# Attention block of a two-block layer on one NeuronCore: value products swapped, on divided probabilities, heads in pairs

## Chip, cores and metric

One core of a Trainium2 chip. The metric is the device time of one execution in microseconds (us), lower is better. The work is in float32, batch 1, 256 tokens, width 2048.

## What is computed

Two blocks, one behind the other. The first has gated linear attention, a convolution branch and a feed-forward layer. The change lies in the second block, and there in its attention of 32 heads of 64: heads 0 to 15 with a T5 bias and dilated masks, 16 to 31 with a neighbourhood bias. With 256 tokens both become a full softmax over 256 keys with a bias and mask.

```python
h = x @ w_in_2                      # q, k, v, gate for heads A and heads B
s = q @ k.T * 64 ** -0.5 + bias     # per head, 256 x 256
p = exp(s - max(s)); den = p.sum(-1)
y = (p @ v / den) * silu(gate)
x = layer_norm(2 ** 0.25 * x + y @ w_out_2) * gain + shift
```

## The kernel before

**Units and steps.** All weight products are cut into 96 units of 512 output columns. A unit has 4 steps of 512 rows each, 384 steps in all (`UNITS`, `NS`). A step s is 24 matmuls of TensorE (`products`, L1190 to L1192): 4 blocks of 128 rows, 2 token tiles, and three products of high and low parts (x_lo w_hi, x_hi w_lo, x_hi w_hi) in fp32r. The weights come by SP's queue into `raw` (three buffers, one load of 1 MB a step). `split(s)` makes `whi` on ScalarE (L604) and `wlo = raw - whi` on VectorE (L849). Each engine does split(s + 2) first in step s, and then the jobs of step s, in order. SP loads step s + 3 after VectorE's split of s.

**Jobs.** `jobs(s)` lists what else a step does. TensorE runs it behind the step's 24 products. `post(u)`, at the last step of unit u, evicts its accumulators `acc`. `turn_...` transposes 8 tiles of the result through two of the four `side` banks of PSUM; ScalarE takes the high part (L609), VectorE the low part (L856). The four banks go round in the order of use: `take` waits until the bank's use four places back has been read.

**Attention.** Units q2, k2, v2 of four groups g (8 heads each) stand at steps 304 to 351, then gates y (352 to 367) and out (368 to 383). Job `att` a runs at 316 + 12 g + (a - 8 g), then a = 32 and 33 at steps 360 and 361. An even a scores heads a and a + 1 (`scores`, L1259 and L1263, three split products with 64 rows each, the two heads in two halves of the array). VectorE adds the bias (L1150) and takes the maximum (L1154, L1157), ScalarE the Exp (L825), in place in `Sm`. Each step a then transposes head a - 1 (`probs`, L1273, 4 tiles in plain f32), ScalarE copies it to `PT` (L820), and the values of head a - 2 follow (`values`, L1286): four plain f32 matmuls, stationary PT (128 x 128), moving `v1`, 64 columns of v and one column of ones that gives the denominator. VectorE divides (L1135, L1138) into `Y`. The gate's post takes Silu on ScalarE (L672), VectorE multiplies by Y (L979), and the product is turned into `A_hi` and `A_lo`. TensorE's order in a step is values, probs, scores, then a turn.

**POOL** fetches the bias of heads a + 2 and a + 3 (`fetch_bias`) after the scores of the same buffer have been read: 2 DMAs (heads below 16) or 4 (L506), then adds the mask (L509).

## Time and profile before

| | us |
|---|---|
| median of 3 runs (2280.4 to 2281.58) | 2281.12 |
| the profiled execution | 2281.08 |
| its span | 2279.3 |
| TensorE busy | 2263.3 (99%) |
| TensorE weight load busy | 1881.8 (83%) |
| VectorE, ScalarE, GpSimd busy | 1215.5, 963.6, 201.0 |

TensorE's granted clock is 0.998 of full. Matmul ends are modelled, so the time that a matmul takes in the stream is read from one start to the next. PE is TensorE, PEld its weight load, DVE VectorE, ACT ScalarE, POOL GpSimd.

### The profile page before, as it was taken

Reading aid. Unit: us, or ns where it says so; the run is one execution under the profiler, and the core shown is the slowest. Engines: PE = TensorE matmul, PEld = TensorE weight load, DVE = VectorE, ACT = ScalarE, POOL = GpSimd, SP = SyncE. Lnnn points to the kernel's source line nnn. Section 1 sums busy time; section 2 is a strip of 40 time slices with the busy share of each in tenths; the row PEclk is TensorE's granted clock in tenths of the full one; section 3 lists DMA queues with packets and bytes.
Section 4 is the critical chain, followed back from the end, with each engine's and each line's share of the span. In section 5 each row is a group of like instructions: output and inputs, shape, how many; then the busy total and the mean of one; then the engine's idle time right before and its main releaser. Section 6 shows DMA issues by size and latency. Waiting matters only on the chain.

```text
span 2279.3 us, 24818 instructions
## 1 busy us (share of the span) xinstructions
PE 2263.3 (99%) x10648; PEld 1881.8 (83%) x10648; DVE 1215.5 (53%) x971; ACT 963.6 (42%) x832; POOL 201.0 (9%) x204
## 2 busy tenths in 40 slices
PE   9999999999999999999999999999999999999997
PEld 7888878888888888888888888888888888888886
DVE  5456535545555544555454454544455555665656
ACT  6444454433344343344433433433444444444532
POOL 1003100000000000000000000000000122253201
PEclk9999999999999999999999999999999999999999
DMA  8545446676666666655555565555556655655663
GB/s 273 185 133 163 148 149 203 194 213 202 202 197 202 204 202 205 219 192 182 192 190 188 186 196 188 184 192 196 185 184 202 243 192 172 189 165 179 211 231 111
DMA packets 213533, 435.60 MB, mean 191 GB/s; under 512 B 8596, under 2 KB 9328, under 8 KB 212528
## 3 DMA queue, kind: packets, MB, share of 16 engines
q1 hardware_dynamic: 205600, 408.98, 55.0%
q0 software_dynamic: 7680, 24.98, 4.6%
q8 instruction: 84, 1.38, 0.2%
q14 instruction: 25, 0.20, 0.0%
q10 hardware_dynamic: 144, 0.07, 0.0%
HBM read 421.93 MB, written 12.06 MB: 190 GB/s over the span
## 4 chain that ended last, share of the span: by engine, by line
PE 98%; DVE 1%; DMA 1%; POOL 0%; ACT 0%; issue 0%; SPq 0%; POOLq 0%; DVEq 0%; ACTq 0%
PE acc L1190 30%; PE acc L1191 30%; PE acc L1192 30%; PE side L1200 2%; PE side L1230 1%; PE side L1286 1%; PE side L1273 1%; PE side L1259 1%; DMA bia<-rb_scratch 0%; DVE X L1018 0%; DVE X L1014 0%; DMA X<-in_x 0%; POOL bia L509 0%; PE side L1350 0%; POOL bia L506 0%
## 5 line engine op out<-in xcount | busy, mean ns | idle before, releaser
L849 DVE TENSOR_TENSOR wlo<-raw,whi 128x2048 fp32r<-128x2048 f32 x382 | 891.4, 2333 | 816.0 <-ACT whi L604 816.0
L604 ACT ACTIVATE whi<-raw 128x2048 fp32r<-128x2048 f32 x382 | 731.6, 1915 | 769.0 <-PE acc L1192 769.0
L1190 PE MATMUL acc<-whi,setA_lo 128*128 128x512 f32 x1792 | 704.4, 393 | 0.1
L1191 PE MATMUL acc<-wlo,setA_hi 128*128 128x512 f32 x1792 | 698.8, 390 | 0.0
L1192 PE MATMUL acc<-whi,setA_hi 128*128 128x512 f32 x1792 | 698.6, 390 | 0.0
L1190 PE MATMUL acc<-whi,setB_lo 128*128 128x512 f32 x1280 | 503.5, 393 | 0.0
L1191 PE MATMUL acc<-wlo,setB_hi 128*128 128x512 f32 x1280 | 498.4, 389 | 0.0
L1192 PE MATMUL acc<-whi,setB_hi 128*128 128x512 f32 x1280 | 498.2, 389 | 0.0
L1190 PEld LDWEIGHTS acc<-whi,setA_lo 128*128 128x128 f32 x1792 | 337.4, 188 | 71.3 <-issue 1.8
L1192 PEld LDWEIGHTS acc<-whi,setA_hi 128*128 128x128 f32 x1792 | 337.3, 188 | 70.3
L1191 PEld LDWEIGHTS acc<-wlo,setA_hi 128*128 128x128 f32 x1792 | 337.4, 188 | 69.4 <-issue 1.0
L1192 PEld LDWEIGHTS acc<-whi,setB_hi 128*128 128x128 f32 x1280 | 240.3, 188 | 50.2
L1190 PEld LDWEIGHTS acc<-whi,setB_lo 128*128 128x128 f32 x1280 | 240.4, 188 | 49.7
L1191 PEld LDWEIGHTS acc<-wlo,setB_hi 128*128 128x128 f32 x1280 | 240.5, 188 | 47.9
L550 POOL TENSOR_TENSOR tmp<-tmp 128x1024 f32<-128x1024 f32 x16 | 30.3, 1896 | 753.5 <-DVE tmp L968 753.5
L609 ACT ACTIVATE setA_hi<-side 128x512 fp32r<-128x512 f32 x48 | 26.1, 595 | 76.6 <-PE side L1200 76.6
L509 POOL TENSOR_TENSOR bia<-bia,msk 128x512 f32<-128x512 f32 x32 | 48.4, 1514 | 81.2 <-DMA bia<-rb_scratch 42.5
L856 DVE TENSOR_TENSOR setA_lo<-side,setA_hi 128x512 fp32r<-128x512 f32 x48 | 30.9, 687 | 38.4 <-ACT setA_hi L609 38.4
L820 ACT ACTIVATE PT<-side 128x512 f32<-128x512 f32 x32 | 19.1, 598 | 75.5 <-PE side L1273 75.5
L1200 PE MATMUL side<-ident,tmp 128*128 128x128 f32 x384 | 49.9, 273 | 0.5 <-DVE Y L1138 0.5
L1200 PEld LDWEIGHTS side<-ident,tmp 128*128 128x128 f32 x384 | 44.4, 140 | 6.7 <-issue 0.7
L543 POOL TENSOR_TENSOR DD<-cum 128x2048 f32<-128x2048 f32 x8 | 33.3, 4161 | 184.6 <-DVE cum L1058 120.6
(181 smaller groups left out, 938.0 us busy)
## 6 DMA issues: line engine op xcount, KB each, us to landing
raw<-in_w_in SPq DMA_DIRECT2D x190, 1024.0 KB, 5.2
raw<-in_w_ffn_up SPq DMA_DIRECT2D x64, 1024.0 KB, 5.3
raw<-in_w_ffn_down SPq DMA_DIRECT2D x64, 1024.0 KB, 5.1
raw<-in_w_gla_out SPq DMA_DIRECT2D x16, 1024.0 KB, 5.1
raw<-in_w_conv_out SPq DMA_DIRECT2D x16, 1024.0 KB, 5.1
raw<-in_w_o SPq DMA_DIRECT2D x16, 1024.0 KB, 5.1
raw<-in_w_out SPq DMA_DIRECT2D x16, 1024.0 KB, 5.1
t_scratch<-t5v POOLq DMA_DIRECT2D x8, 512.0 KB, 7.2
```

Of the source, the lines that this page charges most:

```text
L509: e.tensor_tensor(bia[b][:, :, :], bia[b][:, :, :], msk[h // 16][:, :, :], ALU.add).then_inc(s_mb, 1)
L543: e.tensor_tensor(dv, cv, ref, ALU.subtract).then_inc(s_xd, 1)
L550: e.tensor_tensor(tm, tm, tm, ALU.mult).then_inc(s_pq, 1)
L604: e.activation(whi[r][:, :, :], raw[r][:, :, :], ACT.Copy).then_inc(s_hi, 1)
L609: e.activation(dst[:, 2 * b:2 * b + 2, :], two(side[n % 4][:, :]), ACT.Copy).then_inc(s_th, 1)
L849: e.tensor_tensor(wlo[r][:, :, :], raw[r][:, :, :], asf(whi[r][:, :, :]), ALU.subtract).then_inc(s_lo, 1)
L856: e.tensor_tensor(lo[:, 2 * b:2 * b + 2, :], two(side[n % 4][:, :]), asf(hi[:, 2 * b:2 * b + 2, :]), ALU.subtract).then_inc(s_read[n % 4], 1)
L1190: e.matmul(o, xl, whi[r][:, k, :], start=kk == 0, stop=False)
L1191: e.matmul(o, xh, wlo[r][:, k, :], start=False, stop=False)
L1192: f = e.matmul(o, xh, whi[r][:, k, :], start=False, stop=kk == 15)
L1200: f = e.transpose(bank[:, 256 * j + 128 * t:256 * j + 128 * t + 128], src(t, 2 * b + j), ident[:, :])
L1230: f = e.matmul(bank[:, 128 * h:128 * h + 128], lh[:, j, ss:ss + 128], rh[:, j, t0:t0 + 128], start=dd == 0, stop=dd == 1)
```

## The change

- The value product is swapped: stationary is v (64 columns), moving is the transposed probability, 256 columns. The result is transposed, 64 x 256 per head. It is done as three split products (`vlo` PT, `vhi` PTl, `vhi` PT) in fp32r, for a pair of heads into one bank, in the odd steps, for pair (a - 3) / 2.
- The denominator is the Exp's accumulator output (`den`). `divide` on VectorE takes its reciprocal and divides the probabilities in `Sm`, ahead of the odd step's weight split. The transposes of both heads, a - 2 and a - 1, go to the even steps; ScalarE makes PT (high part), VectorE `PTl`.
- v2's post makes `vhi` on ScalarE and `vlo` on VectorE. The memsets of the column of ones go.
- ScalarE copies the two 64-row halves of a values bank into `YT` (128 channels x 256 tokens per pair).
- The gate is turned alone, before the product. VectorE multiplies it by YT, ScalarE makes A_hi, VectorE A_lo. The gate's turns and those of q2 come one step later, in odd steps.

Left out below: new semaphores, the buffers YT and den, `ready` of out (it waits for A_lo's counter), and POOL's waits (`reload` waits for pair 15 in place of head 31).

```diff
@@ -23,8 +23,8 @@
-         "yb": ("turn_yb",), "wo": ("turn_wo",), "up": ("turn_up",), "q2": ("turn_qk2",), "k2": ("turn_qk2",),
-         "y": ("turn_y",)}
+         "yb": ("turn_yb",), "wo": ("turn_wo",), "up": ("turn_up",), "q2": ("none", "turn_qk2"),
+         "k2": ("turn_qk2",), "y": ("none", "turn_y")}
...
@@ -120,8 +120,10 @@
-        return ([("values", a - 2)] if a >= 2 else []) + ([("probs", a - 1)] if 1 <= a <= 32 else []) \
-            + ([("scores", a), ("scores", a + 1)] if a < 32 and a % 2 == 0 else [])
+        if a % 2:
+            return [("values", (a - 3) // 2)] if a >= 3 else []
+        return ([("probs", a - 2), ("probs", a - 1)] if a >= 2 else []) \
+            + ([("scores", a), ("scores", a + 1)] if a < 32 else [])
...
@@ -234,7 +236,11 @@
-        v1 = [at(f"v1{i}", "W", 4160 * i, [128, 2, 8, 65]) for i in range(2)]
+
+        vhi = [at(f"vhi{g}", "W", 4 * KB * (g % 2), [128, 2, 512], f32r) for g in range(4)]
+        vlo = [at(f"vlo{g}", "A", (16, 20, 16, 24)[g] * KB, [128, 2, 512], f32r) for g in range(4)]
+        PTl = [[at(f"PTl{g}{i}", "A", ((0, 0, 0, 8)[g] + 2 * i) * KB, [128, 2, 256], f32r) for i in range(2)]
+               for g in range(4)]
...
@@ -677,10 +684,11 @@
-                        e.wait_ge(*full("values", 8 * (j - 2) + 7))
+                        e.wait_ge(*full("values", 4 * (j - 2) + 3))
                     e.wait_ge(s_rstd, 3)
-                    e.activation(v1[j % 2][:, 0, :, 0:64], a0[:, :].rearrange("p (h d) -> p h d", d=64), ACT.Copy,
-                                 scale=rstd[2][:, 0:1]).then_inc(ev, 1)
+                    for t in range(2):
+                        e.activation(vhi[j][:, t, :], acc[u % 2][t][:, :], ACT.Copy,
+                                     scale=rstd[2][:, t:t + 1]).then_inc(s_vh, 1)
...
@@ -784,11 +792,18 @@
-                    elif job in ("turn_yb", "turn_up", "turn_y"):
+                    elif job == "turn_y":
+                        j = UNITS[a][1]
+                        e.wait_ge(*set_free(a))
+                        e.wait_ge(s_xf, 2)
+                        e.wait_ge(*full("values", 11 if j < 2 else 15))
+                        for b in range(2):
+                            k = 4 * j + 2 * b
+                            e.wait_ge(*seen("turn", a, b))
+                            e.activation(A_hi[:, k:k + 2, :], YT[:, k:k + 2, :], ACT.Copy).then_inc(s_yh, 1)
+                    elif job in ("turn_yb", "turn_up"):
                         j = UNITS[a][1] % 4
                         e.wait_ge(*set_free(a))
-                        if job == "turn_y":
-                            e.wait_ge(s_xf, 2)
...
@@ -810,20 +825,24 @@
-                        h = a - 1
-                        if 0 <= h < 32:
-                            b = h % 2
+                        if a % 2 and a >= 3:
+                            p = (a - 3) // 2
+                            n = SN["values", p]
+                            e.wait_ge(*full("values", p))
+                            e.activation(YT[0:64, p, :], side[n % 4][0:64, 0:256], ACT.Copy)
+                            e.activation(YT[64:128, p, :], side[n % 4][0:64, 256:512], ACT.Copy).then_inc(s_read[n % 4], 1)
+                        for h in ((a - 2, a - 1) if a >= 2 and a % 2 == 0 else ()):
                             n = SN["probs", h]
                             e.wait_ge(*full("probs", h))
                             if h >= 2:
-                                e.wait_ge(*full("values", h - 2))
-                            e.activation(PT[b][:, :, :], two(side[n % 4][:, :]), ACT.Copy).then_inc(s_read[n % 4], 1)
+                                e.wait_ge(*full("values", h // 2 - 1))
+                            e.activation(PT[h % 2][:, :, :], two(side[n % 4][:, :]), ACT.Copy).then_inc(s_ph, 1)
                         for h in ((a, a + 1) if a < 32 and a % 2 == 0 else ()):
                             b = h % 2
                             e.wait_ge(s_nm, h + 1)
                             for t in range(2):
-                                e.activation(Sm[b][:, t, :], Sm[b][:, t, :], ACT.Exp,
-                                             bias=nmx[b][:, t:t + 1]).then_inc(s_ex, 1)
+                                e.activation(Sm[b][:, t, :], Sm[b][:, t, :], ACT.Exp, bias=nmx[b][:, t:t + 1],
+                                             accum_out=den[b][:, t:t + 1]).then_inc(s_ex, 1)
...
@@ -967,16 +986,12 @@
-                    if j >= 2:
-                        e.wait_ge(*full("values", 8 * (j - 2) + 7))
-                    e.tensor_scalar(v1[j % 2][:, 1, :, 0:64], a1[:, :].rearrange("p (h d) -> p h d", d=64),
-                                    rstd[2][:, 1:2], None, ALU.mult).then_inc(ev, 1)
-                elif kind == "y":
-                    e.wait_ge(*evacuated(u))
-                    e.wait_ge(*seen("values", 8 * j + 7))
+                    if j == 3:
+                        e.wait_ge(*full("scores", 23))
                     for t in range(2):
-                        tm = tmp_of(u)[:, t, :]
-                        e.tensor_tensor(tm, Y[:, t, cols], tm, ALU.mult).then_inc(s_ym, 1)
+                        e.wait_ge(s_vh, 2 * j + t + 1)
+                        e.scalar_tensor_tensor(out=vlo[j][:, t, :], in0=acc[u % 2][t][:, :], scalar=rstd[2][:, t:t + 1],
+                                               in1=asf(vhi[j][:, t, :]), op0=ALU.mult, op1=ALU.subtract).then_inc(ev, 1)
...
@@ -994,6 +1009,17 @@
+            def divide(h):
+                nonlocal dv
+                b = h % 2
+                e.wait_ge(s_ex, 2 * h + 2)
+                e.reciprocal(rd[b][:, :], den[b][:, :]).then_inc(s_dv, 1)
+                dv += 1
+                e.wait_ge(s_dv, dv)
+                for t in range(2):
+                    d = e.tensor_scalar(Sm[b][:, t, :], Sm[b][:, t, :], rd[b][:, t:t + 1], None, ALU.mult)
+                d.then_inc(s_pn, 1)
+
...
@@ -1026,6 +1052,10 @@
+                for job, a in jobs(s):
+                    if job == "att" and a < 32 and a % 2:
+                        divide(a - 1)
+                        divide(a)
...
@@ -1101,7 +1131,18 @@
-                    elif job in ("turn_yb", "turn_up", "turn_y"):
+                    elif job == "turn_y":
+                        j = UNITS[a][1]
+                        e.wait_ge(*seen("values", 4 * j + 3))
+                        for b in range(2):
+                            n = SN["turn", a, b]
+                            k = 4 * j + 2 * b
+                            v = YT[:, k:k + 2, :]
+                            e.wait_ge(*full("turn", a, b))
+                            e.tensor_tensor(v, two(side[n % 4][:, :]), v, ALU.mult).then_inc(s_read[n % 4], 1)
+                            e.wait_ge(s_yh, 2 * j + b + 1)
+                            e.tensor_tensor(A_lo[:, k:k + 2, :], v, asf(A_hi[:, k:k + 2, :]), ALU.subtract).then_inc(s_yl, 1)
...
@@ -1126,18 +1167,14 @@
-                        h = a - 2
-                        if h >= 0:
+                        for h in ((a - 2, a - 1) if a >= 2 and a % 2 == 0 else ()):
                             b = h % 2
-                            n = SN["values", h]
-                            ps = two(side[n % 4][:, 0:130])
-                            e.wait_ge(*full("values", h))
-                            e.reciprocal(rd[b][:, :].unsqueeze(2), ps[:, :, 64:65]).then_inc(s_dv, 1)
-                            dv += 1
-                            e.wait_ge(s_dv, dv)
-                            e.tensor_tensor(Y[:, :, 64 * h:64 * h + 64], ps[:, :, 0:64],
-                                            rd[b][:, :].unsqueeze(2).to_broadcast([128, 2, 64]),
-                                            ALU.mult).then_inc(s_read[n % 4], 1)
+                            n = SN["probs", h]
+                            if h == 0:
+                                e.wait_ge(s_xf, 2)
+                            e.wait_ge(s_ph, h + 1)
+                            e.tensor_tensor(PTl[h // 8][b][:, :, :], two(side[n % 4][:, :]), asf(PT[b][:, :, :]),
...
@@ -1266,7 +1303,7 @@
...
@@ -1274,17 +1311,19 @@
-            def values(h):
-                b, g = h % 2, h // 8
-                e.wait_ge(*seen("probs", h))
-                if h % 8 == 0:
+            def values(p):
+                g, j = p // 4, p % 4
+                for h in (2 * p, 2 * p + 1):
+                    e.wait_ge(*seen("probs", h))
+                if j == 0:
                     e.wait_ge(*evacuated(UI["v2", g]))
-                    e.wait_ge(s_v1, 2)
-                bank, done = take(("values", h))
-                for t in range(2):
+                bank, done = take(("values", p))
+                for i in range(2):
                     for s in range(2):
-                        f = e.matmul(bank[:, 65 * t:65 * t + 65], PT[b][:, s, 128 * t:128 * t + 128],
-                                     v1[g % 2][:, s, h % 8, :], start=s == 0, stop=s == 1)
+                        for n, (x, y) in enumerate(((vlo[g], PT), (vhi[g], PTl[g]), (vhi[g], PT))):
+                            f = e.matmul(bank[0:64, 256 * i:256 * i + 256],
+                                         x[:, s, 128 * j + 64 * i:128 * j + 64 * i + 64],
+                                         y[i][:, s, :], start=s == 0 and n == 0, stop=s == 1 and n == 2)
...
@@ -1362,8 +1401,6 @@
-                        elif kind == "y":
-                            e.wait_ge(s_ym, 2 * j + 2)
                         else:
                             e.wait_ge(*evacuated(a))
                         if kind in ("wo", "down"):
@@ -1373,12 +1410,15 @@
                         for b in range(2):
                             turn(("turn", a, b), b, lambda t, jj: src[:, t, 128 * jj:128 * jj + 128])
                     elif job == "att":
-                        if a >= 2:
-                            values(a - 2)
-                        if 1 <= a <= 32:
-                            probs(a - 1)
-                        if a < 32 and a % 2 == 0:
...
-                            scores(a)
+                        if a % 2:
+                            if a >= 3:
+                                values((a - 3) // 2)
+                        else:
+                            if a >= 2:
+                                probs(a - 2)
+                                probs(a - 1)
+                            if a < 32:
+                                scores(a)
```

## Rows read from the trace of the kernel before

**Rows 1.** The page's chain that ended last: shares of the span by engine.

```profile
PE 98%; DVE 1%; DMA 1%; POOL 0%; ACT 0%; issue 0%; SPq 0%; POOLq 0%; DVEq 0%; ACTq 0%
```

**Rows 2.** TensorE's waits, whole span: line, waited for, us, times, longest.

```profile
PE side L1200 <- DVE Y L1138: 0.5, 1, 0.5
```

**Rows 3.** TensorE's timeline, step 17: start us, us, operation; low-rank product L1328 to L1330.

```profile
115.60 0.39 PE L1192 MATMUL acc<-whi,setA_hi 128*128 128x512 f32 x1
115.83 0.28 PE L1328 MATMUL side<-setA_lo,wlr_hi 128*16 128x256 f32 x1
...
121.45 0.40 PE L1190 MATMUL acc<-whi,setA_lo 128*128 128x512 f32 x1
```

**Rows 4.** TensorE's timeline, jobs of steps 354 and 355, start of job 356.

```profile
2092.04 1.00 PE L1286 MATMUL side<-v,PT 128*128 128x65 f32 x8
2092.88 0.61 PE L1273 MATMUL side<-ident,Sm 128*128 128x128 f32 x4
2093.42 0.38 PE L1259 MATMUL side<-kTa,qTl 64*128 64x256 f32 x1
...
2094.32 0.50 PE L1190 MATMUL acc<-whi,setB_lo 128*128 128x512 f32 x1
...
2099.90 1.00 PE L1286 MATMUL side<-v,PT 128*128 128x65 f32 x8
2100.73 0.61 PE L1273 MATMUL side<-ident,Sm 128*128 128x128 f32 x4
2101.09 0.48 PE L1190 MATMUL acc<-whi,setB_lo 128*128 128x512 f32 x1
...
2106.64 1.00 PE L1286 MATMUL side<-v,PT 128*128 128x65 f32 x8
```

**Rows 5.** TensorE's timeline, the turn of step 360 and what follows.

```profile
2138.46 1.04 PE L1200 MATMUL side<-ident,tmp 128*128 128x128 f32 x8
2139.26 0.48 PE L1190 MATMUL acc<-whi,setB_lo 128*128 128x512 f32 x1
```

**Rows 6.** Groups by form, whole span: count, busy us, mean ns, idle before.

```profile
L1083 DVE TENSOR_SCALAR uu<-zp,VT 128x256 f32<-128x256 f32 x16 | 5.6, 347 | 0.0
...
L639 ACT ACTIVATION_READ_ACCUMULATOR tmp<-X 128x1 f32 x16 | 3.0, 187 | 0.0
...
L727 ACT ACTIVATE lrT<-side 16x256 f32<-16x256 f32 x2 | 0.7, 373 | 12.3 <-PE side L1330 8.6 <-PE side L1342 3.6
```

**Rows 7.** VectorE's timeline, steps 354 and 355; in brackets idle time and releaser.

```profile
2094.43 0.69 DVE L1150 SCALAR_TENSOR_TENSOR Sm<-side,bia 128x512 f32<-128x512 f32 x1 [0.85 <-PE side L1263]
...
2097.29 0.69 DVE L1150 SCALAR_TENSOR_TENSOR Sm<-side,bia 128x512 f32<-128x512 f32 x1 [1.25 <-POOL bia L509]
...
2101.75 3.01 DVE L849 TENSOR_TENSOR wlo<-raw,whi 128x2048 fp32r<-128x2048 f32 x1 [2.78 <-ACT whi L604]
...
2106.62 2.29 DVE L849 TENSOR_TENSOR wlo<-raw,whi 128x2048 fp32r<-128x2048 f32 x1 [0.26 <-ACT whi L604]
```

**Rows 8.** ScalarE's timeline, the post of gate unit 0 in step 355.

```profile
2102.22 1.28 ACT L672 ACT_TABLE_LOAD   x1
2103.51 1.27 ACT L672 ACTIVATE tmp<-acc,rstd 128x512 f32<-128x512 f32 x2
```

**Rows 9.** POOL's timeline, adds of the mask to the bias.

```profile
2095.91 1.29 POOL L509 TENSOR_TENSOR bia<-bia,msk 128x512 f32<-128x512 f32 x1 [4.29 <-DMA bia<-rb_scratch]
...
2101.31 1.29 POOL L509 TENSOR_TENSOR bia<-bia,msk 128x512 f32<-128x512 f32 x1 [1.74 <-DMA bia<-rb_scratch]
...
2115.74 1.27 POOL L509 TENSOR_TENSOR bia<-bia,msk 128x512 f32<-128x512 f32 x1 [3.08 <-DMA bia<-rb_scratch]
...
2122.11 1.27 POOL L509 TENSOR_TENSOR bia<-bia,msk 128x512 f32<-128x512 f32 x1 [2.73 <-DMA bia<-rb_scratch]
```

**Rows 10.** Weight loads of L1286 and L1328: durations min/median/max ns, first and last start.

```profile
L1286 PEld LDWEIGHTS side<-v,PT x256: 187/192/192, 1846.1 to 2145.5; 128*128 128x128 f32 x128
...
L1328 PEld LDWEIGHTS side<-setA_lo,wlr_hi x16: 93/94/95, 115.6 to 121.0; 128*16 128x16 f32 x16
```

More of the change, by code:

```diff
@@ L201, in two_block_program @@
         Sm = [at(f"Sm{i}", "X", 4 * KB + 2 * KB * i, [128, 2, 256]) for i in range(2)]
-        PT = [at(f"PT{i}", "X", 8 * KB + 2 * KB * i, [128, 2, 256]) for i in range(2)]
+        PT = [at(f"PT{i}", "X", 8 * KB + 2 * KB * i, [128, 2, 256], f32r) for i in range(2)]
         msk = [at(f"msk{i}", "X", 12 * KB + 2 * KB * i, [128, 2, 256]) for i in range(2)]
@@ L213, in two_block_program @@
         GA = at("GA", "Y", 0, [128, 2, D])
-        Y = at("Y", "Y", 0, [128, 2, D])
+        YT = at("YT", "Y", 0, [128, 16, 256])
         V = at("V", "V", 0, [128, 2, D])
@@ L254, in two_block_program @@
         nmx = [small(f"nmx{i}", [128, 2]) for i in range(2)]
+        den = [small(f"den{i}", [128, 2]) for i in range(2)]
         rd = [small(f"rd{i}", [128, 2]) for i in range(2)]
@@ L292, in two_block_program @@
         s_zero = sem("s_zero")
-        s_lvl, s_one, s_z, s_scz, s_z0, s_v1 = (sem(n) for n in ("s_lvl", "s_one", "s_z", "s_scz", "s_z0", "s_v1"))
+        s_lvl, s_one, s_z, s_scz, s_z0 = (sem(n) for n in ("s_lvl", "s_one", "s_z", "s_scz", "s_z0"))
         s_sq = [sem(f"s_sq{i}") for i in range(3)]
@@ L299, in two_block_program @@
         s_cu, s_cm, s_ch, s_cv = sem("s_cu"), sem("s_cm"), sem("s_ch"), sem("s_cv")
-        s_yb, s_pq, s_xf, s_ym = sem("s_yb"), sem("s_pq"), sem("s_xf"), sem("s_ym")
+        s_yb, s_pq, s_xf = sem("s_yb"), sem("s_pq"), sem("s_xf")
         s_mb, s_nm, s_ex = sem("s_mb"), sem("s_nm"), sem("s_ex")
+        s_pn, s_ph, s_pl = sem("s_pn"), sem("s_ph"), sem("s_pl")
+        s_vh, s_yh, s_yl = sem("s_vh"), sem("s_yh"), sem("s_yl")
         s_var, s_sd, s_rs, s_nmu = sem("s_var"), sem("s_sd"), sem("s_rs"), sem("s_nmu")
@@ L372, in ready @@
             if kind == "out" and j == 0:
-                return seen("turn", UI["y", kk // 4], part % 2)
+                return s_yl, part + 1
             return None
@@ L561, in pool @@
                             e.dma_start(msk[k][:, :, :], C[name]).then_inc(s_mk, 16)
-                        for b in range(2):
-                            e.memset(v1[b][:, :, :, 64:65], 1.0).then_inc(s_v1, 1)
                     elif job == "bias":
@@ L569, in pool @@
                     elif job == "reload":
-                        e.wait_ge(*full("values", 31))
+                        e.wait_ge(*full("values", 15))
                         e.wait_ge(s_mb, 32)
@@ L1103, in vector @@
                             e.tensor_tensor(B_lo[:, k:k + 2, :], v, asf(B_hi[:, k:k + 2, :]), ALU.subtract).then_inc(s_cv, 1)
-                    elif job in ("turn_yb", "turn_up", "turn_y"):
+                    elif job == "turn_y":
[9 more added lines that the diff above has]
+                            e.tensor_tensor(A_lo[:, k:k + 2, :], v, asf(A_hi[:, k:k + 2, :]), ALU.subtract).then_inc(s_yl, 1)
+                    elif job in ("turn_yb", "turn_up"):
                         j = UNITS[a][1] % 4
@@ L1128, in vector @@
                     elif job == "att":
[L1129 to L1130 removed]
+                        for h in ((a - 2, a - 1) if a >= 2 and a % 2 == 0 else ()):
                             b = h % 2
[L1132 to L1140 removed]
+                            n = SN["probs", h]
[3 more added lines that the diff above has]
+                            e.tensor_tensor(PTl[h // 8][b][:, :, :], two(side[n % 4][:, :]), asf(PT[b][:, :, :]),
+                                            ALU.subtract).then_inc(s_read[n % 4], 1)
                         for h in ((a, a + 1) if a < 32 and a % 2 == 0 else ()):
@@ L1268, in probs @@
                 b = h % 2
-                e.wait_ge(s_ex, 2 * h + 2)
+                e.wait_ge(s_pn, h + 1)
                 bank, done = take(("probs", h))
```

## The prediction

> **What bounds the kernel now.** I read the chain of waits first: 98% of the span lies on TensorE [rows 1]. Its own list of waits says how hard: besides the start-up it waits once, 0.5 us, for VectorE's product of Y and gate [rows 2]. So the order of TensorE's instructions is the time. What an edit takes from this stream, or adds, counts in full. Work on the other engines costs nothing until it makes TensorE wait.
>
> TensorE's timeline gives the prices, each from start to start, since the ends are modelled and overlap. A weight product takes 0.227 us (115.60 to 115.83), so a step of 24 takes 5.44 [rows 3]. Between steps stands the job. From the values of step 354 at 2092.04 to those of step 355 at 2099.90 it is 7.86, so an even job is 2.42. From there to 2106.64 it is 6.74, so an odd job is 1.30 [rows 4]. An even job is values 0.84, transposes and entry into the scores 0.54, scores 0.90, and 0.14 in the first products behind them. An odd one is values 0.83, transposes 0.36, and 0.11 behind. Eight transposes of a turn take 0.80 [rows 5], so four more transposes beside four cost 0.43. Going from plain f32 back to the split products costs 0.1.
>
> **The value products.** A head had four plain f32 matmuls, recorded as eight, in 0.84. A pair of heads has now 2 heads x 2 key halves x 3 products = 12 matmuls with 256 moving columns, 64 stationary columns and fp32r operands. The trace has no such shape. Nearest is the low-rank product, also three fp32r products with 256 moving columns: 48 of them from 115.83 to 121.45, 0.117 each, with no gap on entry or exit [rows 3]. Its stationary side has 16 columns, not 64. So 12 x 0.117 = 1.40 per pair. The bounds: 0.110, what 256 columns more add between 0.117 and 0.227, gives 1.32; 0.134, if a load held its whole recorded duration (94 ns for 16 columns, 188 for 128, so 134 for 64 [rows 10]), gives 1.61. Over 16 pairs that is 1.3 us less or 3.3 us more. I take 0.117, the only row of the same stream and type; it lies 0.023 above its own load's 94.
>
> **The steps.** An even job becomes eight transposes and the scores: 2.42 - 0.84 + 0.43 = 2.01. An odd one becomes the values alone, f32r on both sides, so without the 0.1: 1.40. A pair of steps had 3.72 and has 3.41, so 0.31 goes, 15 times: 4.65. The first odd step loses its transposes and their exit, 0.36 + 0.13, about 0.49. The last two steps had 0.84 + 0.44 + 0.80 + 0.10 and 0.84, and get 0.90, 1.40 and a turn of 0.90: about 0.1 more. The turns of three q units and of gate units 0 and 1 go to odd steps: eight transposes each as before, but the exit of 0.1 is no longer shared with the even job: 0.03 to 0.10 each, I take 0.2 in all. The wait of 0.5 [rows 2] goes, since TensorE now turns the gate before it meets Y. The sum without new waits is 4.65 + 0.49 - 0.1 - 0.2 + 0.5 = 5.4 us.
>
> **What is added beside it.** VectorE: reciprocal and two divides of 128x256 in SBUF (0.35 each, as L1083 [rows 6]) per head, 0.87; the rest PTl of a head's transposes, 0.69 as other 128x512 differences; vlo, eight small ones. Away go the 0.46 per head of L1135 and L1138 and the multiply of Y. ScalarE: an accumulator read of 0.19 behind each of 64 Exps [rows 6], 0.38 a head; two copies of 64x256 into YT per pair, 0.37 or a little more each (L727 [rows 6]), 0.85. None is on TensorE's stream. POOL loses two memsets; its bias DMAs and SP's queue of weights are as before, and the reload of X waits for the same step.
>
> **The new waits.** The divide stands ahead of the odd step's split, and so behind it queue wlo of two steps on, and SP's next load. It waits for the last Exp, behind which ScalarE's split stands anyway. In a usual pair I count from the end of an even step's products (0). Transposes are full at 0.6 and 1.0; ScalarE's copies and PTl end at 2.5; scores evicted from 2.45, the second nmx at 5.6; Exps to 7.0; split on ScalarE to 8.9; VectorE's second divide ends at 7.9, before the split's input is there, so the divide costs nothing; wlo at 11.2, +0.7 where POOL's add holds it. TensorE wants it at 14.3 + 2.0 = 16.3. Five us are spare. The probabilities (divided at 7.9) are wanted at 14.3, PTl (2.5) at 7.4. So nearly everywhere there is no wait, and a q turn of 1.1 on ScalarE, or a q post, fits too.
>
> The tight place is steps 354 to 361, where the gate's posts bring a table load of 1.28 and 1.27 of Silu [rows 8]. There the bias of head 27 is late already: its eviction waits to 2097.29, 5.25 after the step's products, for POOL's add that ended at 2097.20 [rows 7, 9]. As eviction 24, which starts POOL's fetch, stays where it is and the period shrinks by 0.3, it comes at 5.5. The ledger from there, 0 being the end of products 354: nmx 7.2, Exps 8.5, split 357 on ScalarE 10.4 and on VectorE 12.75, copies to YT 11.25, post of y0 13.8, split 358 on ScalarE 15.7, on VectorE 18.05, both PTl 19.35, second nmx 22.5, Exps 23.8, split 359 25.7 and 28.05. Now the gate's turn, which goes to and fro (multiply 0.69, ScalarE 0.6, difference 0.69, twice): second multiply 30.65, second copy 31.25. The scores of head 31 need that bank at about 30.45: 0.2 wait. Split 360 33.15 and 35.5, PTl 36.8 (values of pair 14 want it at 36.92: no wait), second nmx 39.95, Exps 41.25, split 361 43.15 and 45.5; TensorE wants it at 44.65 + 0.2: 0.65 wait. Copies 44.0, post of y1 46.55, split 362 48.45 and 50.75, PTl of head 31 52.05; the last values want it at 50.95: 1.1 wait. That is 1.95 us. One split met by POOL's add, 3.01 in place of 2.29 [rows 7], adds up to 0.7; I take 2.4 for all. Afterwards ScalarE catches up: the turns of y2 and y3 stand alone, and y3's parts are ready 4.7 after products 369, wanted from 6.3.
>
> **The sum.** The profiled execution took 2281.08, 1.8 more than its span and 0.04 less than the median of the runs, so no shift between them. 2281.1 - 5.4 + 2.4 = 2278.1 us, 0.13% less. A difference of 0.2% is 4.6 us, about what a measurement can tell from none.
>
> **A rule against this change.** The loads of 128 stationary columns last 187 to 192 ns in the record, those of 16 columns 94 [rows 10], yet 0.105 and 0.117 pass from start to start, so they run beside a product. The Trainium skill, TensorE: Matmul & The Clock Gate, section Part 3: Packing small matmuls, says that a weight load overlaps a running matmul only if its row group differs, and its section LDWEIGHTS gives columns / 1.2 ns. By that, as an estimate, 64 columns are 53 ns of exposed load in each of 192 matmuls, and the sum would be a loss of 5 us in place of a gain of 5.4. By that rule the trace disagrees: loads of 188 and starts 0.105 apart. Rival 3 is the same mechanism, priced from rows.
>
> **Rivals.**
> (1) The chain in 354 to 361 doesn't get late. For it: the ledger is tight by tenths, and if bias 27 comes 1.4 earlier or the turn's steps overlap better, all three waits shrink to below 0.5. Against it: three table loads lie in this stretch whatever happens. It gives 2281.1 - 5.4 + 0 to 0.5 = 2275.9, and 2274.5 with values at 0.110.
> (2) It gets later. VectorE and POOL hold each other up: a split took 3.01 where POOL's add of 2101.31 ran [rows 7, 9], and the divides are further operations in SBUF while POOL issues its bias loads. Its adds of 2115.74 and 2122.11 are 6.4 apart [rows 9], so 12.7 for two heads. Four divides of 0.35 a pair, if POOL stood still in all of them, make that 14.1, as long as the period. Then each bias after 27 comes later too, and with two splits held the waits are 2.4 + 1.4 + 1.4, about 5.2: 2280.9, no change.
> (3) The other side: the load of 64 columns isn't hidden when matmuls take only 107 ns. Its price from rows: 0.105 from start to start where a load of 128 columns and nearly nothing else passes [rows 4], so half of it, 0.053, on each of 192 products: 10.1 us. That gives 2288.2, and it turns slower by 0.2% from 0.157 us a product on. For it: no row shows 64 columns with 256 moving. Against it: 16 columns and 128 columns both show no such sum.
> (4) The change doesn't do what it says, in that the swapped products are no shorter than the old: 0.134 each makes 1.61 a pair where the old had 1.67, and with the waits that is 2278.1 + 3.3 = 2281.4, no change either.
>
> **How the numbers follow.** The forecast, 2278.1, has 0.48 (its own range 2277.0 to 2279.6); rival 1 0.27; rivals 2 and 4 together 0.19; rival 3 0.06. Faster by over 0.2%, below 2276.6, is rival 1: 0.27. Slower by over 0.2% is rival 3: 0.06. The rest is 0.67. The range of 8 in 10 takes in the better half of rival 1 and rival 2: 2275.0 to 2280.9, and leaves out rivals 3 and 4 and the ends.
>
> **What the profile after would show.** Right: a pair's values take 1.40 from start to start, an odd job without turn is equal to that, an even one 2.01; the period of two steps is 14.3; the waits of TensorE name VectorE's wlo L849 or the PTl difference, each below 1.5 us, all in steps 358 to 361; the divide stands in VectorE's idle time before the split. Wrong: values at 0.13 or more; TensorE waits in earlier pairs, for wlo or the divided probabilities; no wait at 361 (rival 1); or evictions of scores that wait for the bias in most pairs (rival 2).

## The result, and the profile after

| us | before | changed |
|---|---|---|
| median of the runs | 2281.35 (14 runs) | 2277.12 (14 runs) |
| lowest and highest | 2280.4, 2282.26 | 2273.66, 2278.23 |
| the profiled execution, its span | 2281.08, 2279.3 | 2276.67, 2274.9 |

The ratio is 0.998, with an interval of 0.9973 to 0.9988: 4.2 us or 0.19% less. The forecast was 2278.1, with a range of 2275.0 to 2280.9. Executions of either kernel lie at times some 3 us below the rest (two of these 14, at 2273.66 and 2273.97), and one of experiment 1 took 7063.17 and is left out of its median; no trace of such a one exists, so the cause stays open.

The page of the changed kernel, busy times and the chain that ended last, against the table of before and [rows 1]:

```profile
PE 2258.8 (99%) x10584; PEld 1874.4 (82%) x10584; DVE 1254.0 (55%) x1039; ACT 984.0 (43%) x932; POOL 202.0 (9%) x202
...
PE 99%; DVE 1%; DMA 0%; SPq 0%; issue 0%; ACT 0%; DVEq 0%
```

VectorE has 38.5 us more work and ScalarE 20.4 more, yet the span shrank by 4.4: TensorE's busy time fell by 4.5, and the chain still runs along TensorE. Its waits in the changed kernel, whole span (line, waited for, us, times, longest), which answer [rows 2]:

```profile
PE side L1237 <- DMA X<-in_x: 2.4, 2, 1.9
PE acc L1242 <- DVE tmp L862: 1.5, 1, 1.5
PE side L1324 <- issue: 0.2, 1, 0.2
```

The first two are the start-up, hundreds of steps ahead of the change. The third is all that this list shows of the 32 heads; how much it costs the stream is read below from the starts (0.4). The 0.5 for Y is gone.

The jobs of steps 354 and 355 on TensorE's timeline, as [rows 4] shows them for before (start, us, operation):

```profile
2088.46 1.03 PE L1310 MATMUL side<-ident,Sm 128*128 128x128 f32 x8
2089.43 0.38 PE L1296 MATMUL side<-kTa,qTl 64*128 64x256 f32 x1
...
2090.32 0.50 PE L1227 MATMUL acc<-whi,setB_lo 128*128 128x512 f32 x1
...
2095.94 0.28 PE L1324 MATMUL side<-PT,vlo 128*64 128x256 f32 x1
2096.05 0.28 PE L1324 MATMUL side<-PTl,vhi 128*64 128x256 f32 x1
...
2097.30 0.40 PE L1227 MATMUL acc<-whi,setB_lo 128*128 128x512 f32 x1
...
2102.78 1.03 PE L1310 MATMUL side<-ident,Sm 128*128 128x128 f32 x8
```

The even job runs from 2088.46 to 2090.32, 1.86, and 0.17 more hidden in the first products: products take from 2090.32 to 2095.94, 5.62, where a step of them is 5.44 [rows 3]. The odd job runs from 2095.94 to 2097.30: twelve value products in 1.36, 0.114 each, and 0.03 behind. The next even job starts at 2102.78, so two steps take 14.32.

For a balance I take the stretch from the first scores to the last gate turn, which leaves out the start-up. Before it is 350.80 (1833.91 to 2184.71). In the changed kernel it is 351.70 (1834.06 to 2185.76) with one step of 5.44 more in it, since the last turn stands a step later, so 346.26. The attention gained 4.54 us. Every experiment below is held against 351.70. Outside the stretch even equal code differs: the first scores start at 1834.06 here and at 1834.76 in a second profile of the same kernel (experiment 12). That is why the stretch is the finer measure.

### The profile page after: what moved, and what is told of

The parts are those of the page before. It is cut to its first block, busy times and chain, and to the rows that moved or that the text cites. A ratio compares the mean times of both kernels' runs of the same rounds, so it can differ in the third digit from the quotient of the medians.

```text
span 2274.9 us, 24851 instructions
## 1 busy us (share of the span) xinstructions
PE 2258.8 (99%) x10584; PEld 1874.4 (82%) x10584; DVE 1254.0 (55%) x1039; ACT 984.0 (43%) x932; POOL 202.0 (9%) x202
## 4 chain that ended last, share of the span: by engine, by line
PE 99%; DVE 1%; DMA 0%; SPq 0%; issue 0%; ACT 0%; DVEq 0%
PE acc L1227 31%; PE acc L1228 31%; PE acc L1229 31%; PE side L1237 2%; PE side L1267 1%; PE side L1324 1%; PE side L1296 1%; PE side L1310 1%; DVE X L1044 0%; DVE X L1040 0%; DMA X<-in_x 0%; PE side L1389 0%; PE side L1279 0%; PE side L1282 0%; PE side L1281 0%; PE side L1369 0%
## 5 line engine op out<-in xcount | busy, mean ns | idle before, releaser
L844 ACT ACTIVATE Sm<-Sm,nmx 128x256 f32<-128x256 f32 x64 | 32.1, 502 | 49.4 <-DVE nmx L1194 49.4
L515 POOL DMA_DIRECT2D bia<-rb_scratch x64 | 39.1, 618 | 64.9 <-DVE Sm L1187 63.4
```

What stands on the lines that cost most here:

```text
L515: e.dma_start(dst, src).then_inc(s_bia[b], 16)
L844: e.activation(Sm[b][:, t, :], Sm[b][:, t, :], ACT.Exp, bias=nmx[b][:, t:t + 1], accum_out=den[b][:, t:t + 1]).then_inc(s_ex, 1)
```

## Experiments

Timed runs were made beside the kernel before, whose medians were 2281.35 to 2281.86.

**1. Is the place ahead of the split worth anything?** In VectorE's step the two lines change places.

```diff
+                if s + 2 < NS:
+                    split(s + 2)
                 for job, a in jobs(s):
                     if job == "att" and a < 32 and a % 2:
                         divide(a - 1)
                         divide(a)
-                if s + 2 < NS:
-                    split(s + 2)
```

> The changed kernel with one move: VectorE divides behind the odd step's weight split. Theory (slack everywhere but in steps 357 to 361): in a usual pair the divided probabilities are ready about 1.7 us later than now and are still wanted later, so no wait; in the stretch of the gate turns VectorE's chain grows by 1.7 us per pair, TensorE's waits of 0.6 us there become 2 to 4 us, and the time is 2278.5 to 2280.5. Rival (the place of the divide doesn't matter anywhere, since VectorE is free again before TensorE asks): 2277.1, within 0.5.

Measured: 2281.75, ratio 0.9999 (0.999 to 1.0008), stretch 356.78, 5.1 longer. TensorE's waits in the stretch, and VectorE's timeline at the pair that loses most:

```profile
PE side L1310 <- DVE Sm L1020: 2.0, 1, 2.0
PE side L1296 <- DVE YT L1142: 1.2, 1, 1.2
PE side L1296 <- DVE qTl L875: 0.6, 1, 0.6
PE side L1237 <- DVE tmp L949: 0.3, 1, 0.3
```

```profile
2135.08 2.29 DVE L868 TENSOR_TENSOR wlo<-raw,whi 128x2048 fp32r<-128x2048 f32 x1 [2.97 <-ACT whi L611]
2137.29 0.16 DVE L1016 RECIPROCAL rd<-den 128x2 f32<-128x2 f32 x1
2137.49 0.61 DVE L1020 TENSOR_SCALAR Sm<-Sm,rd 128x256 f32<-128x256 f32 x2
```

VectorE idles 2.97 us ahead of the split, since the split's input comes from ScalarE behind both Exps, and the divide then stands behind 2.29 of split. In the changed kernel the same place reads so:

```profile
2127.25 0.16 DVE L1016 RECIPROCAL rd<-den 128x2 f32<-128x2 f32 x1
2127.45 0.61 DVE L1020 TENSOR_SCALAR Sm<-Sm,rd 128x256 f32<-128x256 f32 x2
2128.51 0.17 DVE L1016 RECIPROCAL rd<-den 128x2 f32<-128x2 f32 x1 [0.45 <-ACT Sm L844]
2128.71 0.62 DVE L1020 TENSOR_SCALAR Sm<-Sm,rd 128x256 f32<-128x256 f32 x2
2130.31 2.29 DVE L868 TENSOR_TENSOR wlo<-raw,whi 128x2048 fp32r<-128x2048 f32 x1 [0.99 <-ACT whi L611]
```

Both divides fit in, and 0.99 of idle time is left. So the divide ahead costs nothing, and without that place the whole gain of the change is lost. Comparing the starts of the jobs one by one, nearly all of the loss falls at four places: 1.05 behind the first q turn (step 322), 0.5 at the k turn of step 324, 1.3 in step 358, 2.2 and 0.35 in step 360, less 0.37 for a wait that the changed kernel has at the end. The other pairs lose hundredths, some 0.1 in all. I had the kind right, the size (1.5 to 3.5) too small, and the 1.5 at the two turns of the first group nowhere.

**2. What are the turns in odd steps worth?**

```diff
-         "yb": ("turn_yb",), "wo": ("turn_wo",), "up": ("turn_up",), "q2": ("none", "turn_qk2"),
-         "k2": ("turn_qk2",), "y": ("none", "turn_y")}
+         "yb": ("turn_yb",), "wo": ("turn_wo",), "up": ("turn_up",), "q2": ("turn_qk2",),
+         "k2": ("turn_qk2",), "y": ("turn_y",)}
```

> The changed kernel with the turns of q and gate back in the even steps, behind the scores. Theory (a turn in the odd step costs TensorE one more exit from plain f32, 0.03 to 0.1 us, and the gate's turn in step 357 is what makes the chain late): five turns give back 0.1 to 0.5 us, the waits of 0.6 at step 361 vanish, time 2276.2. Rival (the odd step was needed because ScalarE and VectorE are full after the scores of an even step): waits of 1 to 3 us appear in even steps with a turn, time 2278 to 2280.

Measured: 2279.21, ratio 0.9988 (0.9979 to 0.9997). The stretch is 348.04, with the step of 5.44 added 353.48: 1.8 longer. TensorE's waits, and the longest on its timeline:

```profile
PE side L1237 <- DVE PTl L1176: 2.1, 4, 1.6
```

```profile
2107.51 1.16 PE L1237 MATMUL side<-ident,tmp 128*128 128x128 f32 x8 [1.60 <-DVE PTl L1176]
```

A turn in the even step stands behind four other uses of the banks, and takes one whose transposed probabilities VectorE must still read for PTl, which stands behind its split. In an odd step that read is long past. My expectation of 2276.2 was wrong: the wait at step 361 does vanish, but the new ones cost more. The rival's time is right; its reason (both engines full) is narrowed by the list to one read of one bank.

**3. The type of the value products.** Plain f32 operands, four matmuls per pair in place of twelve.

```diff
-                        for n, (x, y) in enumerate(((vlo[g], PT), (vhi[g], PTl[g]), (vhi[g], PT))):
+                        for n, (x, y) in enumerate(((vhi[g], PT),)):
...
-        PT = [at(f"PT{i}", "X", 8 * KB + 2 * KB * i, [128, 2, 256], f32r) for i in range(2)]
+        PT = [at(f"PT{i}", "X", 8 * KB + 2 * KB * i, [128, 2, 256]) for i in range(2)]
...
-        vhi = [at(f"vhi{g}", "W", 4 * KB * (g % 2), [128, 2, 512], f32r) for g in range(4)]
+        vhi = [at(f"vhi{g}", "W", 4 * KB * (g % 2), [128, 2, 512]) for g in range(4)]
```

> The changed kernel with the swapped value product in plain f32, as the kernel before had it unswapped: 4 matmuls a pair, each recorded as two. Theory (a plain f32 pass with 256 moving columns costs two streams, as 16 of the low-rank gate took 3.65 us, 0.228 each): 8 x 0.213 to 0.228 = 1.70 to 1.82 in place of 1.37 a pair, plus 0.1 exit; 16 x 0.45 = 7 us more, 2284 us: the swap alone is a loss, and the split products in fp32r make it a gain. Rival (a pass costs 0.107 whatever the type, as 65 columns took 0.105): 16 x (0.86 + 0.1 - 1.40) = 7 less, 2270.

Measured: 2287.23, ratio 1.0022 (1.0012 to 1.0031), stretch 362.05. TensorE's timeline, one odd job:

```profile
2103.99 0.39 PE L1229 MATMUL acc<-whi,setB_hi 128*128 128x512 f32 x1
2104.31 1.94 PE L1324 MATMUL side<-PT,vhi 128*64 128x256 f32 x8
2106.18 0.50 PE L1227 MATMUL acc<-whi,setB_lo 128*128 128x512 f32 x1
```

Four plain matmuls are recorded as eight and take 1.87, 0.234 each; twice 0.114 is 0.228. So one plain f32 product of this shape costs over four fp32r ones, and three split products beat it: 0.5 per pair, 8 of the 10.35. The rest lies in the joints with the neighbours. Behind the values it is 0.14 in place of 0.03, in the 11 pairs where no turn follows: 1.2. Ahead of them the last product of the step lasts 0.32 (2103.99 to 2104.31) in place of 0.23, in all 16: 1.5. That is 10.7, less the 0.4 of the wait at the end, which this kernel hasn't: 10.3 for 10.35. My expectation had the direction right and 3 us too little, since it took each recorded entry at 0.213 to 0.228 and left out the joint ahead. Against the kernel before, the swap in plain f32 is 5.6 us slower.

**4. The other way: one product in place of three.** The two products with low parts are left out.

```diff
-                        for n, (x, y) in enumerate(((vlo[g], PT), (vhi[g], PTl[g]), (vhi[g], PT))):
+                        for n, (x, y) in enumerate(((vhi[g], PT),)):
```

> The changed kernel with only the product of the high parts in the values: 4 of 12 matmuls a pair; the two products with a low part are left out. Theory (TensorE's stream is the time, a product is 0.114 us from start to start): 16 x 8 x 0.114 = 14.6 us less, 2262.5. Rival (another engine's chain is close behind in the attention): the gain stops early, at 5 us or less, 2272, and TensorE shows waits in most pairs.

Measured: 2266.80, ratio 0.9935 (0.9921 to 0.9948), stretch 340.98, 10.7 shorter. TensorE's timeline and its wait:

```profile
2085.82 0.62 PE L1324 MATMUL side<-PT,vhi 128*64 128x256 f32 x4
2086.28 0.40 PE L1227 MATMUL acc<-whi,setB_lo 128*128 128x512 f32 x1
```

```profile
PE side L1296 <- DVE YT L1142: 2.4, 1, 2.4
```

A pair takes 0.46 in place of 1.37, which is 14.6 over 16 pairs; 3.9 of it comes back in steps 358 to 361: TensorE waits 4.3 there (2.6 in the first job, of which its list names 2.4, and 1.6 on the next ones), of which the changed kernel has 0.4 too. So the theory had the price of the products right and left out the waits (2262.5), and the rival stopped the gain too early (2272). The gate's stretch runs near the limit of VectorE and ScalarE, and a shorter period makes it late.

**5. The table loads of the gate.** Copy in place of Silu in the posts of the gate.

> The changed kernel with Copy in place of Silu in the four posts of the gate: the gate's nonlinearity is left out, and with it ScalarE's table loads between Exp and Silu in steps 355, 356 and 359. Theory (the waits at step 361 are the end of a chain on ScalarE and VectorE in which each table load counts 1.28): the chain ends 2.5 to 3.8 us earlier, TensorE's waits of 0.6 there vanish, the time falls by that, to 2276.5. Rival (the waits come from the bias or from the bank of the turn, not from ScalarE): both waits stay as they are.

Measured: 2276.34, ratio 0.9976 (0.9966 to 0.9985), stretch 351.29, 0.4 shorter, and no wait of TensorE in the attention. All that the table loads cost is the one wait at the end, as expected.

**6. Scores ahead of the transposes in the even steps.**

```diff
-                            if a >= 2:
-                                probs(a - 2)
-                                probs(a - 1)
                             if a < 32:
                                 scores(a)
+                            if a >= 2:
+                                probs(a - 2)
+                                probs(a - 1)
```

> The changed kernel with the scores ahead of the two transposes in each even step. TensorE's instructions are the same. Theory (entering and leaving the half-array scores next to plain f32 costs 0.17 + 0.17 now; from the f32r products straight into them it costs less): an even job falls from 2.04 to about 1.89, 15 times, 2.3 us in all, 2274.8. The transposes end 0.9 us later and with them PTl and the eviction of the scores, which the usual pair has to spare, and step 361's waits grow to at most 1.5. Rival (the place of an exit doesn't change its price, and the later transposes cost): 2277 to 2279.

Measured: 2278.0, ratio 0.9983 (0.9974 to 0.9991), stretch 351.93. TensorE's timeline, an even job, and its waits:

```profile
2086.47 0.39 PE L1229 MATMUL acc<-whi,setB_hi 128*128 128x512 f32 x1
2086.78 0.38 PE L1296 MATMUL side<-kTa,qTl 64*128 64x256 f32 x1
...
2087.69 1.09 PE L1310 MATMUL side<-ident,Sm 128*128 128x128 f32 x8
2088.53 0.48 PE L1227 MATMUL acc<-whi,setB_lo 128*128 128x512 f32 x1
```

```profile
PE side L1324 <- issue: 0.6, 1, 0.6
PE side L1324 <- DVE Sm L1187: 0.5, 1, 0.5
PE side L1310 <- DVE YT L1142: 0.2, 1, 0.2
```

The job itself shrinks from 1.86 to 1.75, and the joint behind it from 0.17 to 0.11. But the scores now follow the products, and the last product ahead of them lasts 0.31 (2086.47 to 2086.78) in place of 0.23: this joint of 0.09 takes back half, and a pair of steps takes 14.23 for 14.32. The 1.4 that this makes over the stretch is lost again in steps 358 to 361, where TensorE waits 2.0 in place of 0.4. My expectation of 2274.8 was wrong. The rival's time (2277 to 2279) is right; of its two reasons the later transposes hold, while the price of the joint did move with the order.

**7. A longer divide.** Two more passes by 1.0 over the probabilities ahead of each reciprocal, four operations of 0.35 per head.

> The changed kernel with two more passes over the probabilities in each head's divide (times 1.0), 1.4 us a head on VectorE ahead of the odd step's split. Theory (5 us are spare in a usual pair, none at 361): the split of the odd step comes 1.9 to 2.4 us later in all 16 pairs, TensorE waits in none of the first 12, and in steps 358 to 361 the delays of two pairs add up to about 4 us: 2281. Rival (the divide is on the way of each pair): 16 x 2 us, 2309.

Measured: 2279.28, ratio 0.999 (0.9981 to 0.9999), stretch 353.79, 2.1 longer. TensorE's waits in the stretch:

```profile
PE side L1302 <- DVE YT L1148: 1.5, 1, 1.5
PE acc L1233 <- DVE wlo L868: 0.4, 1, 0.4
```

Both lie in the gate's steps; from 1830 to 2100 us TensorE doesn't wait at all. So a usual pair takes 2.8 us more of VectorE for nothing, as its 5 us of room in the forecast said. Only the last pairs have no room, and there the delay cost half of what I expected (2.1 for 4).

**8. Shorter dependence in the gate's turn.** VectorE makes both multiplies first, then both low parts, so that it doesn't go to and fro with ScalarE.

```diff
                             e.tensor_tensor(v, two(side[n % 4][:, :]), v, ALU.mult).then_inc(s_read[n % 4], 1)
+                        for b in range(2):
+                            k = 4 * j + 2 * b
+                            v = YT[:, k:k + 2, :]
                             e.wait_ge(s_yh, 2 * j + b + 1)
```

> The changed kernel with VectorE's work of a gate turn in another order: both multiplies first, then both low parts, in place of one after the other. Theory (the to-and-fro between VectorE and ScalarE in step 357 carries the chain to step 361): it ends 1.4 us earlier, TensorE's waits of 0.6 vanish, 2276.5. Rival (the split of step 361 is late for ScalarE's Exps and tables alone): the waits stay.

Measured: 2276.42 (2275.78 to 2277.19), ratio 0.9978 (0.9969 to 0.9987), stretch 351.37, 0.33 shorter, no wait of TensorE in the attention. It takes off the last wait, as expected, and does so although POOL's bias for head 27 came 0.5 later in this profile than in that of the changed kernel. Against the changed kernel 0.7 us or less is too little to be told surely by the medians; the stretch and the list of waits are what speaks for it.

**9. Both, 6 and 8.**

> Scores first and both multiplies first together, on the changed kernel. Theory (the two add up: the pair of steps falls from 14.32 to 14.23, as with the scores first alone, and the shorter work of the gate's turn takes most of the 2.4 us of waits that the late transposes brought in steps 358 to 361): 15 x 0.09 = 1.4 less than with both multiplies alone plus 0.5 to 1.5 of waits, 2275.5 to 2276.5, so no gain over it that a measurement tells. Rival (the waits vanish too): 2275.0.

Measured: 2276.66, ratio 0.9978 (0.9969 to 0.9987), stretch 351.20, with waits of 0.6 and 0.2 at the last pairs. No better than 8 alone, as expected, and a little above the 2275.5 to 2276.5 that I gave.

**10. Is the weight load hidden?** All 128 columns of the two heads as stationary operand, each head's half of the result used.

```diff
-                            f = e.matmul(bank[0:64, 256 * i:256 * i + 256],
-                                         x[:, s, 128 * j + 64 * i:128 * j + 64 * i + 64],
+                            f = e.matmul(bank[:, 256 * i:256 * i + 256],
+                                         x[:, s, 128 * j:128 * j + 128],
```

> The changed kernel with 128 stationary columns in each value product: the v of both heads, half of the result unused, so the same 12 products with twice the weight load. Theory (the load runs beside the product before it): 1.37 us for a pair's values as now, 2277.1. Rival (the load is in part exposed, columns / 1.2 ns by the Trainium skill, TensorE: Matmul & The Clock Gate, section LDWEIGHTS, an estimate of 53 ns for 64 more columns; in rows, half of the 0.105 that a load of 128 and 65 moving columns took, 0.053): 12 x 0.053 = 0.63 more a pair, 10.1 in all, 2287.2.

Measured: 2278.36, ratio 0.9985 (0.9976 to 0.9994), stretch 352.90. TensorE's timeline of one odd job, and the durations of the loads (min/median/max ns) in the changed kernel and in this one:

```profile
2098.24 0.28 PE L1324 MATMUL side<-PT,vlo 128*128 128x256 f32 x1
...
2099.67 0.40 PE L1227 MATMUL acc<-whi,setB_lo 128*128 128x512 f32 x1
```

```profile
L1324 PEld LDWEIGHTS side<-PT,vlo x64: 132/134/135, 1853.3 to 2140.0; 128*64 128x64 f32 x64
```

```profile
L1324 PEld LDWEIGHTS side<-PT,vlo x64: 186/192/192, 1854.8 to 2142.7; 128*128 128x128 f32 x64
```

The load grew by 58 ns in the record, the product by 5: twelve take 1.43 in place of 1.37. Loads of 134 and of 192 ns both run beside products 0.114 and 0.119 apart, and both are longer than that distance. This settles rival 3. If the load stood in the stream at 0.053 per 64 columns, this kernel would be 10 us slower; it is 1.2 in the stretch, 1.0 from the products and 0.2 from a longer wait at step 361. So the rule that the prediction held against the change isn't borne out here.

**11. Scores first only in the early pairs** (heads below 26), with 8: where there is room, take the shorter joint; where there is none, leave the order.

> Both multiplies first, and the scores ahead of the transposes in the even steps before 354 alone, where the chain has time to spare. Theory (the dearer exit counts in every pair, the waits of the scores first only in the last three): 12 pairs of 14.23 and no waits at steps 358 to 361: 1.1 us less than with both multiplies alone, 2275.3. Rival (the first late transposes reach the tight stretch): waits as with both together, 2276.7.

Measured: 2277.09, ratio 0.9978 (0.9969 to 0.9987), stretch 351.53. The joint is won in 12 pairs, and steps 360 and 361 wait again, 1.3 in all (0.6 at the values, 0.2 for wlo, the rest at loads). The tight pairs are reached with less ahead: POOL's add of bias 27 ends 6.3 after the products of step 354, where it ends 4.7 in the changed kernel and 5.3 in experiment 8. In 4, 6 and 9, whose pairs are shorter too, it ends 6.0 to 6.3 after them. My expectation of 2275.3 was wrong, and the rival's right.

**12. The changed kernel once more**, beside 11.

> The changed kernel itself, on the same chip as the version before it, to compare the two there: 2277.1, a wait of 0.4 to 1 us for PTl at step 361.

Measured: 2277.49, ratio 0.9984 (0.9975 to 0.9993), stretch 351.89, and again one wait of some 0.6 at step 361. So the stretch repeats within 0.2.

## Why the forecast held, and where it was off

**The value products: right.** I took 0.117 from the low-rank product [rows 3]; it is 0.114, a pair 1.37 + 0.03 for 1.40. The load lasts 134 ns, just as interpolated between [rows 10]. Experiment 10 shows that it is hidden, 3 and 4 that the price follows the number and type of the products.

**Even and odd jobs: nearly right.** 2.04 for 2.01 and 1.40 for 1.40, a pair of steps 14.32 for 14.29. That 0.03 is 15 x 0.03 = 0.45 in all. It is most of what parts the saving without new waits, 4.9 (4.54 and the 0.4 of waits), from the forecast's 5.4. The terms of that sum add up to 5.34, so 0.06 of the gap is an error of addition.

**The divide: right.** It stands in idle time of VectorE, which 1 and 7 show from both sides. ScalarE's two additions cost what was taken or a little less (two copies 0.75 a pair for 0.85), in the changed kernel by groups (busy us, mean ns):

```profile
L1020 DVE TENSOR_SCALAR Sm<-Sm,rd 128x256 f32<-128x256 f32 x64 | 24.8, 430 | 1.2
...
L844 ACT ACTIVATION_READ_ACCUMULATOR Sm<-Sm,nmx 128x1 f32 x64 | 11.9, 186 | 0.0
...
L833 ACT ACTIVATE YT<-side 64x256 f32<-64x256 f32 x16 | 6.0, 376 | 0.2
```

The divide's mean is 430 where I took 350; its median is 352, and single ones reach 1483. The long ones run beside POOL's adds, here two divides in place of 0.62:

```profile
1853.09 1.75 DVE L1020 TENSOR_SCALAR Sm<-Sm,rd 128x256 f32<-128x256 f32 x2
```

```profile
1853.13 1.30 POOL L518 TENSOR_TENSOR bia<-bia,msk 128x512 f32<-128x512 f32 x1 [2.49 <-DMA bia<-t_scratch]
```

That is rival 2's mechanism at work, but in pairs with room: no wait of TensorE follows from it.

**The waits in steps 354 to 361: the right place, the wrong size.** This is the term of the sum that was mis-sized: 2.4 forecast, 0.4 measured. TensorE at step 361, and VectorE ahead of it:

```profile
2138.41 0.39 PE L1229 MATMUL acc<-whi,setB_hi 128*128 128x512 f32 x1
2139.01 0.30 PE L1324 MATMUL side<-PT,vlo 128*64 128x256 f32 x1 [0.21 <-issue]
```

```profile
2135.42 2.29 DVE L868 TENSOR_TENSOR wlo<-raw,whi 128x2048 fp32r<-128x2048 f32 x1 [2.81 <-ACT whi L611]
2137.62 1.28 DVE L1176 TENSOR_TENSOR PTl<-side,PT 128x512 fp32r<-128x512 f32 x2
```

The last product of step 361 starts at 2138.41, and the values would follow 0.2 later; they start at 2139.01, when the second PTl has been done for 0.1. So the wait costs the stream 0.4, which is also what 5 and 8 gain without it. TensorE's list gives it only as 0.2; the weight load's own shows 0.6, waiting for `PTl L1176`. It is the third wait of my ledger, with PTl done 50.4 after products 354 in place of 52.05. The other two didn't come: split 361 was done at 44.1 where I had 45.5 and TensorE wanted it at 44.65, and the gate turn's second bank was free at 29.8 where I had 30.65 and it was wanted at 30.5.

The fault begins in the first line of the ledger. POOL's add of bias 27, in the changed kernel:

```profile
2091.90 1.29 POOL L518 TENSOR_TENSOR bia<-bia,msk 128x512 f32<-128x512 f32 x1 [3.30 <-DMA bia<-rb_scratch]
```

It ends at 2093.19, 4.7 after the products of step 354 (2088.46), and the eviction behind it starts at 4.8. I had moved that to 5.5, from 5.25 in before [rows 7], because the period shrinks. The add waited 3.30 for its DMA where before it waited 4.29, so the transfer landed sooner; why it did, these runs don't tell. It scatters too: the same code up to this point has the add end at 4.7, 4.9, 5.1 and 5.3 in the profiles of the changed kernel, 12, 5 and 8.

These 0.7 run through the whole ledger, and it was tight by tenths. To them each pass through ScalarE adds a little: Exps 1.14 for 1.3, copies to YT 0.65 for 0.85, since an instruction can start 0.1 before the record of the one ahead ends. At ScalarE's split of step 359 that makes 1.6 (24.1 for 25.7), and at the last PTl 1.6 again, the collision below having cost 0.7 in between. As two waits fell away, TensorE also wanted that PTl 0.8 earlier than the ledger said, which is why 0.4 of the third wait was left.

**The collision with POOL** that I priced at up to 0.7 did happen. The split of step 359 and POOL's add beside it, in the changed kernel:

```profile
2112.57 3.02 DVE L868 TENSOR_TENSOR wlo<-raw,whi 128x2048 fp32r<-128x2048 f32 x1 [0.99 <-ACT whi L611]
```

```profile
2112.16 1.28 POOL L518 TENSOR_TENSOR bia<-bia,msk 128x512 f32<-128x512 f32 x1 [2.29 <-DMA bia<-rb_scratch]
```

It takes 3.02 in place of 2.29, and TensorE doesn't wait where it falls. But it leads the chain: the gate's multiply follows it without idle time, ScalarE's copies and its split of step 360 wait for the multiply, and so on to the PTl of step 361. By these links the 0.7 is more than the whole wait of 0.4 there. No run takes the collision away alone, so this is read from the links and not shown by experiment.

**The sum.** 2281.08 - 4.54 is 2276.5 for the profiled execution of 2276.67. What happened is my rival 1 by its mechanism (the chain hardly gets late), and lies between its time and the forecast: it too had waits of 0 to 0.5, but a saving of 5.4 where 4.9 were made. Rivals 2 and 4 fell with the timelines, rival 3 with experiment 10. The forecast of the time was near because the part that carried it, prices by start to start on the bounding engine, was sound; the ledger's 2.0 too many waits was its error, and 0.5 too much saving and 0.45 between the profiled run and the median partly offset it. That these two lean the other way is luck: it puts the median 0.1 inside the forecast's own range of 2277.0 to 2279.6, where the profiled run lies outside it.

Of the variants that compute the same only 8 has no wait left in the attention and steady times, at 2276.42. What is left in this stretch is TensorE's own work and its joints.

## What to carry to other kernels

Where one engine is busy 99% of the time, price an edit by the distance from start to start of the nearest row of the same stream and type, and write a ledger of the others only for the stretch that has least room; give that ledger's first entry a range, since its tenths run through all the rest, and put a collision into the chain where it falls. Work added to a second engine is free if it goes ahead of an instruction that waits for something later anyway: the same divide cost nothing there and 5 us behind it, nearly all at four places. Ordering for a cheaper joint (6, 9, 11) gains little when the next tight stretch takes it back, so remove the tight wait first.

## What the runs showed of the hardware

- A plain f32 product costs over four times an fp32r one of the same shape: four took 1.87 where twelve fp32r ones took 1.37, 256 columns each.
- Weight loads of 64 and 128 columns last 134 and 192 ns in the record, though the products beside them start only 0.114 and 0.119 apart: the 64 further columns cost 0.005 a product.
- Changing between kinds of matmuls has a price that moves with the order. Behind a job it is 0.03 after the fp32r values, 0.14 after the same values in plain f32, 0.10 to 0.14 after transposes and 0.17 after the scores, which use two halves of the array. Ahead of a job it is 0.09 before the scores (experiment 6) and before the plain f32 values of experiment 3, and nothing before transposes or fp32r values.
- VectorE and POOL hold each other up: a split took 3.02 beside POOL's add and 2.29 without, two divides 1.75 beside an add and 0.62 without, and an add 2.79 beside a split (2083.43) and 1.29 without.
